# Softmax weights of the attention heads: one of two transpose batches moved into the middle of the next projection, and the next group's scores put ahead of the other

## The reference, cut to what matters

```python
s = (jnp.einsum('bhqd,bhkd->bhqk', qb, k) * scale + cb[..., None] - c[:, :, None, :])
s = jnp.where(kpos[None, :] <= qpos[:, None], s, -jnp.inf)
p = jax.nn.softmax(s, axis=-1)
return jnp.einsum('bhqk,bhkd->bhqd', p, v)
```

## Time and profile before

| what | value |
|---|---|
| median of three runs | 1595.7 us (1590.94, 1595.7, 1596.18) |
| span of the profiled execution (first to last instruction) | 1593.9 us |
| own time of the profiled execution | the page gives its span alone; it lies among the three runs, 1.8 us under their median |
| PE busy | 1489.7 us (93%) |
| DVE / ACT busy | 1165.7 us (73%) / 989.1 us (62%) |
| share of PE in the chain that ended last | 80% |
| mean granted TensorE clock | 0.971 |
| steps k = 8 to 11, layer 0 | about 111 to 147 us |
| steps k = 8 to 11, layer 1 | about 499 to 534 us |

### The profile page before, as it was taken

One profiled execution on the slowest core, in us unless ns is written; L12 is line 12 of the kernel. 1 busy time (PEld: TensorE's weight loads), 2 busy tenths in 40 slices (PEclk: granted clock), 3 DMA queues, 4 the chain that ended last, 5 costly groups with the idle time before them and its releaser, 6 DMA issues.

```text
span 1593.9 us, 21108 instructions
## 1 busy us (share of the span) xinstructions
PE 1489.7 (93%) x8033; PEld 1260.3 (79%) x8033; DVE 1165.7 (73%) x921; ACT 989.1 (62%) x876; POOL 92.7 (6%) x103
## 2 busy tenths in 40 slices
PE   7989799997898969999999999999999999999993
PEld 7988499997897748887887887887887887888882
DVE  4873445544576357888888888888888888888884
ACT  6454244443736227777777777777777777777772
POOL 4221000000031111000000000000000000000001
PEclk9999899999899979999999999999999999999997
DMA  8421596543333159999999999999999999999983
GB/s 256 160 106 54 173 322 205 185 137 128 107 108 110 48 198 344 386 375 348 394 379 339 395 372 349 393 372 350 391 372 355 388 369 351 388 378 373 392 319 105
DMA packets 211785, 449.19 MB, mean 282 GB/s; under 512 B 12884, under 2 KB 37016, under 8 KB 211736
## 3 DMA queue, kind: packets, MB, share of 16 engines
q1 hardware_dynamic: 210584, 444.31, 77.1%
q0 software_dynamic: 1152, 4.19, 0.7%
HBM read 433.80 MB, written 14.68 MB: 281 GB/s over the span
## 4 chain that ended last, share of the span: by engine, by line
PE 80%; DVE 8%; ACT 8%; issue 3%; DMA 1%; POOL 0%; ACTq 0%; DVEq 0%; POOLq 0%; SPq 0%
PE bank L1357 24%; PE bank L1359 23%; PE bank L1358 23%; DVE low L1210 3%; ACT high L875 2%; PE bank L1581 2%; PE bank L1568 2%; PE bank L1665 1%; ACT winh L708 1%; PE bank L1482 1%; DVE QD L982 1%; PE bank L1409 1%; ACT XN L676 1%; ACT results L869 1%; ACT L898 1%
## 5 line engine op out<-in xcount | busy, mean ns | idle before, releaser
L1210 DVE TENSOR_TENSOR low<-raw,high 128x2048 fp32r<-128x2048 f32 x336 | 768.2, 2297 | 131.2 <-ACT high L875 130.7
L875 ACT CAST high<-raw 128x2048 fp32r<-128x2048 f32 x336 | 642.8, 1917 | 187.2 <-PE bank L1359 187.2
L1357 PE MATMUL bank<-high,xeh 128*128 128x512 f32 x896 | 355.1, 396 | 6.6 <-DVE low L1210 6.6
L1359 PE MATMUL bank<-high,xel 128*128 128x512 f32 x896 | 349.6, 390 | 0.0
L1358 PE MATMUL bank<-low,xeh 128*128 128x512 f32 x896 | 349.0, 389 | 0.0
L1357 PEld LDWEIGHTS bank<-high,xeh 128*128 128x128 f32 x896 | 168.3, 188 | 45.2 <-DVE low L1210 12.1
L1359 PEld LDWEIGHTS bank<-high,xel 128*128 128x128 f32 x896 | 168.2, 188 | 36.1
L1358 PEld LDWEIGHTS bank<-low,xeh 128*128 128x128 f32 x896 | 168.4, 188 | 33.4
L1357 PE MATMUL bank<-high,hdh 128*128 128x512 f32 x448 | 175.2, 391 | 7.8 <-DVE hdl L1310 7.8
L1359 PE MATMUL bank<-high,hdl 128*128 128x512 f32 x448 | 174.4, 389 | 0.0
L1358 PE MATMUL bank<-low,hdh 128*128 128x512 f32 x448 | 174.3, 389 | 0.0
(11 more groups left out here) (289 smaller groups left out, 1990.9 us busy)
## 6 DMA issues: line engine op xcount, KB each, us to landing
raw<-in_moe_w_gate_dram SPq DMA_DIRECT2D x112, 1024.0 KB, 7.3
raw<-in_moe_w_up_dram SPq DMA_DIRECT2D x112, 1024.0 KB, 7.3
raw<-in_moe_w_down_dram SPq DMA_DIRECT2D x112, 1024.0 KB, 7.2
ring<-in_w_in_dram SPq DMA_DIRECT2D x10, 2048.0 KB
dring<-in_dense_w_gate_dram SPq DMA_DIRECT2D x5, 2048.0 KB
dring<-in_dense_w_up_dram SPq DMA_DIRECT2D x5, 2048.0 KB
dring<-in_dense_w_down_dram SPq DMA_DIRECT2D x5, 2048.0 KB
ring<-in_w_in_dram SPq DMA_DIRECT2D x8, 1024.0 KB
```

Of the source, the lines that this page charges most:

```text
L875: act.copy(high[:, q % SPLIT, :], raw[:, q % RAW, :]).then_inc(s_hi, 1)
L1210: dve.tensor_tensor(low[:, q % SPLIT, :], raw[:, q % RAW, :], high[:, q % SPLIT, :].bitcast(F32), ALU.subtract).then_inc(s_lo, 1)
L1357: pe.matmul(o, xh, wh, start=first, stop=False)
L1359: return pe.matmul(o, xl, wh, start=False, stop=last)
```

## The change: what it does

The two transpose batches of a group become two calls, on PE and on ACT.

- On PE batch 0 now stands after the scores of the next group, where both batches stood ahead of them. Batch 1 stands in the next step's `project`, between its two groups of 24 matmuls.
- On ACT the copy of batch 0 keeps its place. The copy of batch 1 moves into the next step, behind `attn_exp` of the next group and ahead of `evacuate`.

No instruction is added or dropped, and no operand or semaphore count changes. DVE, POOL and SP have the same lists as before.

```diff
-            def attn_turned(l, g):
-                for p in range(2):
-                    act.wait_ge(s_tp, 6 * l + 2 * g + p + 1)
-                    if g:
-                        act.wait_ge(s_pv, 3 * l + g)
-                    act.copy(PT[:, p * 512:p * 512 + 512], ps[6][:, :]).then_inc(s_te, 1)
+            def attn_turned(l, g, p):
+                act.wait_ge(s_tp, 6 * l + 2 * g + p + 1)
+                if g:
+                    act.wait_ge(s_pv, 3 * l + g)
+                act.copy(PT[:, p * 512:p * 512 + 512], ps[6][:, :]).then_inc(s_te, 1)
...
                     if k >= 8 and k - 8 < 3:
                         attn_exp(l, k - 8)
+                    if 9 <= k:
+                        attn_turned(l, k - 9, 1)
                     evacuate(l, k + 2)
...
                     if 9 <= k:
                         attn_out(l, k - 9)
                     if k >= 8 and k - 8 < 3:
-                        attn_turned(l, k - 8)
+                        attn_turned(l, k - 8, 0)
...
-            def project(l, i):
+            def project(l, i, between=None):
...
+                    if f == 0 and between is not None:
+                        between()
                 ins.then_inc(s_pp, 1)
...
-            def attn_turn(l, g):
+            def attn_turn(l, g, p):
                 pe.wait_ge(s_pn, 3 * l + g + 1)
-                for p in range(2):
-                    if 2 * g + p:
-                        pe.wait_ge(s_te, 6 * l + 2 * g + p)
-                    for b in range(4):
-                        v = (4 * p + b) * P
-                        ins = pe.transpose(ps[6][:, b * P:(b + 1) * P], PP[g % 2][:, v:v + P], ident[:, :])
-                    ins.then_inc(s_tp, 1)
+                if 2 * g + p:
+                    pe.wait_ge(s_te, 6 * l + 2 * g + p)
+                for b in range(4):
+                    v = (4 * p + b) * P
+                    ins = pe.transpose(ps[6][:, b * P:(b + 1) * P], PP[g % 2][:, v:v + P], ident[:, :])
+                ins.then_inc(s_tp, 1)
...
-                    project(l, k + 2)
+                    project(l, k + 2, (lambda: attn_turn(l, k - 9, 1)) if k >= 9 else None)
...
                     if k >= 9:
                         attn_apply(l, k - 9)
-                    if 8 <= k < 11:
-                        attn_turn(l, k - 8)
                     if 7 <= k < 10:
                         attn_scores(l, k - 7)
+                    if 8 <= k < 11:
+                        attn_turn(l, k - 8, 0)
```

## The result

The changed kernel has a median of 1581.6 us against 1595.65 for the kernel before: ratio 0.9917, 95% interval 0.9900 to 0.9934. One of its four executions took 2228.47 us, at a granted clock of 0.627 over its whole length; it is counted in that median and left out of the ratio, and the other three (1578.12, 1580.15, 1583.04) have their median at 1580.15. A later set of six executions gives 1580.88 and 0.9918 (0.9897 to 0.994). The forecast was 1583.5, faster by over 0.3%.

A forecast was written before the change was run, and what follows sets the result against it. PE, holding 80% of the chain, was taken as the bound. Stages of 30.00 against 36.02 and 29.43 against 35.30 us gave 11.9 us less: 1582.0 from the profiled execution, 1583.8 from the median; forecast 1583.5, range 1579 to 1589.5.

The forecast's parts named there:

- Scores ahead of batch 0: PE: scores wait for the earlier group's exponentials, not its weights, starting 1.17 us after the level in layer 0, 0.60 in layer 1.
- Batch 1 between the halves: PE, within the projection: batch 1 doesn't wait for batch 0's copy and costs 0.41 us, at most 0.66.
- The new wait: Ahead of the first apply, step 9, both layers: PE waits 0.81 us for ACT's chain, 7.58 against PE's 6.77.
- The table loads: ACT: a switch costs 1.28 us; by the skill page's extra 1380 ns drain the wait would be 3.6 us, the time 1589.
- Step 10: Second apply: ACT's copy of batch 1 ends at T + 8.9, PE comes at T + 10.0; no wait, 1.1 us spare.
- The clock: Both stages: 3.0 of the 11.9 us gained are work no longer run at the lower clock behind gaps.
- Rival 2: Both stages: the clock falls all the same, both slow stretches return at 3.0 us, 1586.8; chance 0.16.
- 3: Steps 9 and 10: ACT's chain longer by one or two loads' length, 3 or 8 us in all, middle 1589; chance 0.09.
- 4: Behind the stage: the gain is taken back by something PE doesn't release, 1595.7, within 0.3%; chance 0.08.
- 5: Twelve projection halves of the stage: clock stays low, 1.7 to 3.0 us each, all twelve give 1611; chance 0.05.

The follow-up runs named there:

- the experiment at step 8: Changed kernel with two one-element activations, bringing two more table loads, behind the Silu of `MC` on ACT: 1592.62 us, 0.9989.
- the loads added at step 9: Changed kernel with two one-element activations and their table loads behind the copy of batch 1 of group 0, ahead of the evacuation: 1584.54 us, 0.9944.
- the fill: Kernel before, its order kept, with 14 matmuls nobody reads in PE's list at each of two long gaps per layer: 1591.04 us, 0.9983.
- the kernel with the copy first: Changed kernel with ACT's copy of batch 1 ahead of the next group's exponentials: 1580.21 us, 0.9919; again on another chip 1580.72 us, 0.9917.
- the kernel before again: Kernel before, unchanged, run once more for a second trace: 1593.38 us.

## Why the prediction was right

**Size and place.** 30.00 and 29.43 us were forecast for the stages, 29.87 and 29.35 measured; 11.9 us in all, 12.1 measured. That layer 0 fits so well holds some luck: the sum has a wait of 0.57 ahead of its scores that was there in this trace and not in the next one of the same kernel, whose stage is 29.37. A span of 1582.0 was forecast, 1581.3 measured. One reading was wrong without harm: I took the page's span of 1593.9 for the execution's own time and its distance of 1.8 to the median for scatter. It is what lies around a span: the profiled execution of the changed kernel took 1583.04 with a span of 1581.3, 1.7 more.

**Scores ahead of batch 0.** They start 1.17 us behind the level in layer 0 (111.30 to 112.47) and 0.64 in layer 1, as in the sum (1.17 and 0.60). What the prediction did not say is how little this edit is worth beside the other. It gave the two one sum; alone they are 0.9952 and 0.9909, together 0.9918. Both remove the 1.84 behind the cast, and in both the granted clock in the stages is 1.00; so that part of the gain is counted in each of them, and the gains don't add. The 0.68 of bank 6 goes with the split alone, the wait for the weights with the new place of the scores alone.

**Batch 1 between the halves.** Priced at 0.41 with 0.66 as the upper bound. Batch 0, projection and batch 1 take 132.06 - 125.29 = 6.77 us, just the 0.41 + 6.36 of the sum. Four transposes between matmuls cost what they cost at the head of a group.

**The new wait.** Forecast 0.81 ahead of the first apply, released by ACT; the rows mark 0.58 and 0.60. They count from a modelled end, the forecast from start to start. In that measure ACT's chain took 7.43 (114.65 to 122.08) where I had 7.58, and PE's side takes 6.77 where nothing waits (125.29 to 132.06), as in the sum: 0.66 against 0.81. The trace of the changed kernel has that chain nearly whole:

```profile
115.34 0.59 ACT L746 COPY attention<-bank 128x512 f32<-128x512 f32 x1 [0.66 <-PE bank L1451]
115.95 1.28 ACT L813 ACT_TABLE_LOAD   x1
117.25 1.06 ACT L813 ACTIVATE MC<-MC 128x1024 f32<-128x1024 f32 x1
118.32 1.28 ACT L737 ACT_TABLE_LOAD   x1
119.62 0.47 ACT L737 ACTIVATE XN<-bank,nmx 128x256 f32<-128x256 f32 x1
...
121.43 0.60 ACT L746 COPY attention<-bank 128x512 f32<-128x512 f32 x1
```

The piece that I had longer is from the first exponential to the copy: 121.43 - 119.62 = 1.81 against 1.93. The two experiments on it hold it from both sides: with the copy out of the chain the wait is 0, with 3.0 us more in the chain it is 3.6.

**The table loads.** The switches cost 1.28 us each, and the operation behind one starts 0.02 us after its end (115.95 + 1.28 to 117.25, 118.32 + 1.28 to 119.62); ahead of a load it is 0.02 or less as well (115.34 + 0.59 to 115.95, 117.25 + 1.06 to 118.32). The 1380 ns of drain that the Trainium skill gives with each switch (ScalarE: Activation LUTs, What ACT_TABLE_LOAD costs) are in neither, nor in the three loads of the experiment at step 8, which start right behind one another's activations. The estimate by that page of the Trainium skill, 1589, was over 7 us too slow.

**Step 10.** Spare 1.1 forecast, 1.6 measured: the copy of batch 1 starts at 129.88 with 0.60 in the trace of the changed kernel, and the apply at 132.06; the loads added at step 9 say the same, 3.0 - 1.4.

**The clock.** 3.0 us were forecast as its part, taken from one trace. It was shown nearly apart from the waits with the fill: 2.9 us of the stages, 0.9983; the one trace of that kernel could be chance, but the interval of its twelve executions lies under 1 as well. Rival 2, that it falls all the same, did not come: the granted clock is 1.00 in both stages of the two traces of the changed kernel. Of all twelve traces, 24 stages, a low stretch stands in five: four of the kernel before, with gaps of up to 1.96 us, and one of the two with 3.6 us of waiting. In the other 19 the longest gap is 3.6 once and at most 1.4 otherwise.

**The other rivals.** 3: the chain of ACT was shorter, not longer. 4: nothing was taken back, by the 7.29 and 7.30 us ahead of the output projection. 5: the projections of both stages ran at 1.00.

## What to carry to other kernels

Where two batches go through one bank by turns (PE fills, ACT empties), don't issue them in a row: put other work of PE between them, longer than the hand-over (here 2.97 us against 1.33), and the wait is gone at the price of the batch alone. Then look at what the engine that empties the bank has in its list ahead of the copy: here two table switches with a Silu between them, 3.6 us, and the exponentials stood there, and putting the copy ahead of the second switch and the exponentials was enough to end the wait, 0.5 us of each stage, too little to be told in the time. Price two edits of one stage each alone as well as together, since either may remove the same wait; and count with a gap of PE what the clock takes behind it, here 1.3 to 1.6 us each time it fell behind one of 1.8 to 2 us, and 2.7 us behind one of 3.6.

## What I had not expected of the hardware

**The low clock moves about.** All four stages in two traces of the kernel before have one low stretch, but not behind the same gap; a gap of 3.6 us brought it in one layer and not in the other; and outside the stage it comes and goes from execution to execution. In the changed kernel it is low, for one, in the stretch from 65:

```profile
65.00:70.00 5.00, 5.00 (x32) 4.26 (x32) 3.93 (x6) 3.54 (x4) 1.30 (x1) 0.74 0.00 0
```

in the kernel with the copy first the same stretch is at full clock:

```profile
65.00:70.00 5.00, 5.00 (x42) 4.36 (x42) 3.92 (x6) 3.50 (x4) 1.39 (x1) 1.00 0.00 0
```

When the stage of layer 0 begins goes with this stretch in all twelve traces: at 108.7 to 109.0 in the four that have 1.00 there, at 110.9 to 111.6 in the eight that have 0.73 to 0.90. Not every low stretch has a price: five traces have one between 15 and 30 us, and the stage begins at 108.71 in one of these (the split alone) and at 108.80 in the kernel before again, which has none.

The first wait of a stage goes with the clock as well. It is the longer one (1.96 us for the weights, or 0.46 for the exponentials where the scores stand first) in five stages of the 24, and these are the five with a low stretch some 15 us ahead of them, from 95 to 100 or between 475 and 485 us. So 0.8 us of the 36.02 of before (2.67 against 1.87 from the level to batch 0) came with the clock too, beside the 1.47. How the one brings the other was not followed up.

The executions of one kernel differ in the same way. In the five of the kernel with the copy first, the mean granted clock is 0.977 at 1577.66 and 1579.18 us and 0.970 and 0.969 at 1582.78 and 1582.95. An edit of 1 us can be read in the stage, not in the time. What decides in a given execution stays open.

**Work that nobody needs made a kernel faster**, by 0.17% (0.9983; the interval ends at 0.9993), with 56 matmuls added in two stages.
